# The modulation of a two-block transformer: from TensorE products to running sums on VectorE and GpSimd

## The reference, cut to what matters

```python
silu_c = jax.nn.silu(c)                 # 1 x 1024
silu_cc = jax.nn.silu(c_ctx)            # 1024
for l in range(2):
    mx = jnp.split((silu_c @ w_mod[l] + b_mod[l])[:, None, :], 6, axis=-1)    # w_mod[l] is 1024 x 6144
    mc = jnp.split(silu_cc @ w_mod[l] + b_mod[l], 6, axis=-1)
    zx = modulate(rms_norm_2(x, norm1_g[l]), mx[0], mx[1]) @ w_in[l]
    ...
```

## Time and profile before

| | |
|---|---|
| Median of 3 runs | 3625.23 us (3624.39 to 3630.41) |
| The profiled execution's own time | 3626.35 us |
| Its span, from first to last instruction | 3624.6 us |
| Mean granted TensorE clock | 0.996 |
| Busy: TensorE matmul, weight load | 97%, 74% |
| Busy: VectorE, ScalarE, GpSimd | 47%, 38%, 0% |
| The two stages with the modulation | from about 645 to 1023 us and from about 1649 to 2029 us |

### The profile page before, as it was taken

How to read it: one execution, slowest core, us unless ns; L and a number is a source line. 1 busy time by engine, 2 the same in 40 slices (tenths; PEclk the granted TensorE clock), 3 DMA queues, 4 the chain that set the end, 5 groups by cost and what they waited for, 6 DMA issues and landing times.

```text
span 3624.6 us, 47267 instructions
## 1 busy us (share of the span) xinstructions
PE 3527.7 (97%) x17969; PEld 2669.8 (74%) x17969; DVE 1721.4 (47%) x2508; ACT 1387.3 (38%) x2058; POOL 3.4 (0%) x11
## 2 busy tenths in 40 slices
PE   8999999999999989999999899999999999999999
PEld 5565788777775657887777765488888885469998
DVE  6674434433466754344334555543323355644334
ACT  5554323322245543233222334533322334443334
POOL 0000000000000000000000000000000000000000
PEclk9999999999999999999999999999999999999999
DMA  4121233555532222335555310022222221013332
GB/s 127 54 62 50 84 90 108 145 155 148 145 101 58 57 58 79 93 115 156 149 164 155 81 49 3 2 58 65 64 64 63 59 82 58 4 51 95 93 93 88
DMA packets 576207, 310.28 MB, mean 86 GB/s; under 512 B 28400, under 2 KB 566976, under 8 KB 576064
## 3 DMA queue, kind: packets, MB, share of 16 engines
q1 hardware_dynamic: 575792, 308.18, 30.3%
q10 hardware_dynamic: 272, 0.13, 0.0%
HBM read 297.26 MB, written 2.10 MB: 83 GB/s over the span
## 4 chain that ended last, share of the span: by engine, by line
PE 93%; DVE 3%; ACT 2%; issue 1%; DMA 0%; SPq 0%; DVEq 0%; ACTq 0%
PE ps L1111 14%; PE ps L1112 14%; PE ps L1113 14%; PE ps L1420 10%; PE ps L1422 10%; PE ps L1424 10%; PE ps L1608 2%; PE ps L1590 2%; PE ps L1301 2%; PE ps L1270 1%; PE ps L1195 1%; PE ps L1282 1%; PE ps L1549 1%; PE ps L1298 1%; PE ps L1276 1%
## 5 line engine op out<-in xcount | busy, mean ns | idle before, releaser
L1772 ACT ACTIVATE whi<-wraw 128x1024 fp32r<-128x1024 f32 x448 | 470.7, 1052 | 552.4 <-DMA wraw<-in_w_mlp 247.2
L1111 PE MATMUL ps<-uhi,whi 128*128 128x512 f32 (+1 forms) x1456 | 613.5, 421 | 12.5 <-DVE ulo L2431 5.4
L2414 DVE TENSOR_TENSOR wlo<-wraw,whi 128x1024 fp32r<-128x1024 f32 x448 | 546.0, 1219 | 109.1 <-ACT whi L1772 104.2
L1112 PE MATMUL ps<-ulo,whi 128*128 128x512 f32 (+1 forms) x1456 | 572.7, 393 | 0.0
L1113 PE MATMUL ps<-uhi,wlo 128*128 128x512 f32 (+1 forms) x1456 | 572.5, 393 | 0.0
L1111 PEld LDWEIGHTS ps<-uhi,whi 128*128 128x128 f32 x1456 | 274.2, 188 | 103.0 <-issue 38.6
L1112 PEld LDWEIGHTS ps<-ulo,whi 128*128 128x128 f32 x1456 | 274.7, 189 | 72.3 <-issue 16.3
L1113 PEld LDWEIGHTS ps<-uhi,wlo 128*128 128x128 f32 x1456 | 273.8, 188 | 65.4
L1420 PE MATMUL ps<-u2hi,whi 128*128 128x512 f32 (+1 forms) x1216 | 295.6, 320 | 3.3 <-DVE wlo L2414 2.4
L1420 PE MATMUL ps<-yhi,whi 128*128 128x512 f32 (+1 forms) x976 | 295.9, 353 | 0.0
L1422 PE MATMUL ps<-ylo,whi 128*128 128x512 f32 (+1 forms) x976 | 294.9, 353 | 0.0
(11 more groups left out here) (329 smaller groups left out, 4567.9 us busy)
## 6 DMA issues: line engine op xcount, KB each, us to landing
wraw<-in_w_in SPq DMA_DIRECT2D x128, 512.0 KB, 3.8
wraw<-in_w_mlp SPq DMA_DIRECT2D x128, 512.0 KB, 4.0
mod_raw<-in_w_mod SPq DMA_DIRECT2D x96, 512.0 KB, 5.3
wraw<-in_w_mlp_in SPq DMA_DIRECT2D x64, 512.0 KB, 4.2
wraw<-in_w_mlp_out SPq DMA_DIRECT2D x64, 512.0 KB, 3.9
wraw<-in_w_branch SPq DMA_DIRECT2D x16, 512.0 KB, 3.4
wraw<-in_w_out SPq DMA_DIRECT2D x16, 512.0 KB, 3.8
wraw<-in_w_o SPq DMA_DIRECT2D x16, 512.0 KB, 3.7
```

Source lines behind the costliest of these rows:

```text
L1111: pe.matmul(bank, whs[:, i], x_hi[:, k], start=(i == 0), stop=False)
L1112: pe.matmul(bank, whs[:, i], x_lo[:, k], start=False, stop=False)
L1772: act.activation(whi[:, r], wraw[:, r], ACT.Copy).then_inc(w_hi, 1)
L2414: dve.tensor_tensor(wlo[:, r], wraw[:, r], whi[:, r].bitcast(F32), ALU.subtract).then_inc(w_split, 1)
```

## The change

The sum over the 1024 rows of `w_mod` is split: over the 8 feature tiles k it is made as multiply-and-add of whole tiles (128 x 384), with the partition's value of the condition as a scalar; over the 128 partitions it is made by six transposes on TensorE and a `tensor_reduce` over 128 values on VectorE. VectorE makes the sum for the first condition (one multiplication, then seven `scalar_tensor_tensor`, each behind the one before), GpSimd that for the second (one multiplication, then seven pairs of multiplication and addition, each step behind the one before: 15 steps a group). The loads are now pieces of 3, 3 and 2 feature tiles with all 384 columns (rows of 1536 bytes); SyncE waits for VectorE's sums of the piece (`mod_added`) before it loads the next group's piece into its place. VectorE takes piece b after chunk b = 0, 1, 2, once GpSimd has done with it (`mod_step`). TensorE turns both sums (six transposes, banks `SCORE` and `SCORE + 1`) after chunk b = 3, once both are whole; GpSimd begins the next group behind that (`mod_turned`). The sums lie in `acc`, which is free during the MLP. `mod_kept` now counts the `tensor_reduce` of each group, and TensorE waits for it ahead of the next use of the banks.

```diff
--- before.py
+++ after.py
@@ -84,6 +84,8 @@
 
 UNIT_START, UNIT_SPACE = 18, 2.85
 MOD_GROUP = 3
+MOD_PIECES = ((0, 3), (3, 6), (6, 8))
+MOD_STEPS = 2 * 8 - 1
 BRANCH_TILES = {"diff": (0, 1, 2, 3), "ret": (11, 8, 9, 10), "gqa": (4, 5, 6, 7)}
 BRANCH_KINDS = "diff", "ret", "gqa"
 RET_UNITS, RET_SCORES = (25, 30), (119.5, 134)
@@ -625,7 +627,7 @@
         par_dw = sb("par_dw", [P, DEPTH * TAPS * 2])
         mod = sb("mod", [P, DEPTH, MOD_COLS, 2])
         silu = sb("silu", [P, KT, 2])
-        silu_parts = sb("silu_parts", [P, KT, 32])
+        silu_parts = sb("silu_parts", [P, KT, 2])
 
         one_scope = ExitStack()
         h = sb("h", [P, KT, SEQ], scope=one_scope)
@@ -686,9 +688,10 @@
         sb("place_of_fsq", [P, SEQ], scope=merge_scope)
         sgm = sb("sgm", [P, 2, SEQ], scope=merge_scope)
         acc = sb("acc", [P, 2, SEQ], scope=merge_scope)
+        mod_sums = acc[:, :, SEQ - MOD_GROUP * P:SEQ]
         mst = sb("mst", [P, 2, SEQ], scope=merge_scope)
-        mod_raw = sb("mod_raw", [P, MOD_GROUP, KT, P], scope=merge_scope)
-        mod_rows = sb("mod_rows", [P, MOD_GROUP * P], scope=merge_scope)
+        mod_raw = sb("mod_raw", [P, KT, MOD_GROUP * P], scope=merge_scope)
+        mod_part = sb("mod_part", [P, MOD_GROUP * P], scope=merge_scope)
         merge_scope.close()
         one_scope.close()
 
@@ -795,7 +798,8 @@
         second_in, static_in, dft_in = sem("second_in"), sem("static_in"), sem("dft_in")
         silu_sig_ready, silu_ready = sem("silu_sig_ready"), sem("silu_ready")
         mod_in = [sem(f"mod_in{b}") for b in range(MOD_GROUP)]
-        mod_made, mod_kept, mod_turned = sem("mod_made"), sem("mod_kept"), sem("mod_turned")
+        mod_step, mod_kept, mod_turned = sem("mod_step"), sem("mod_kept"), sem("mod_turned")
+        mod_added = sem("mod_added")
         ring_done, mid_evac = sem("ring_done"), sem("mid_evac")
         early_done, early_added, early_squared = sem("early_done"), sem("early_added"), sem("early_squared")
         early_summed, early_normed, early_log = sem("early_summed"), sem("early_normed"), sem("early_log")
@@ -947,10 +951,11 @@
                                 sp.dma_start(wraw[:, r, :].rearrange("p (k c) -> p k c", c=P), src)\
                                   .then_inc(raw_in[r], 16)
                                 if w_mod is not None and n:
-                                    c = P * MOD_GROUP * (2 * KT // RAW * q + i) + P * (MOD_GROUP * KT // RAW * half + n - 1)
-                                    made = MOD_GROUP * (2 * KT // RAW * q + i)
-                                    sp.wait_ge(mod_made, made + (l * MOD_COLS + MOD_GROUP * KT // RAW * half + n))
-                                    sp.dma_start(mod_raw[:, n - 1], w_mod[:, :, bass.ds(c, P)])\
+                                    group = 2 * KT // RAW * q + i + KT // RAW * half
+                                    k, end = MOD_PIECES[n - 1]
+                                    sp.wait_ge(mod_added, KT * group + (MOD_COLS // MOD_GROUP * KT * l + end))
+                                    sp.dma_start(mod_raw[:, k:end],
+                                                 w_mod[:, k:end, bass.ds(MOD_GROUP * P * group, MOD_GROUP * P)])\
                                       .then_inc(mod_in[n - 1], 16)
 
                 if w_mod is not None and l == DEPTH - 1:
@@ -1083,9 +1088,31 @@
                                pattern=[[-1, P]], channel_multiplier=1).then_inc(pool_const, 1)
             pool.wait_ge(pool_const, 3)
             pool.memset(rotated[:, :], 0.0).then_inc(rotated_clear, 1)
-            pool.wait_ge(mod_turned, 2 * KT // RAW * QUARTERS)
+            groups = MOD_COLS // MOD_GROUP
+
+            def mod_products(l):
+
+                for g in range(groups * l, groups * (l + 1)):
+                    pool.wait_ge(mod_turned, g + 1)
+                    for b, (first, end) in enumerate(MOD_PIECES):
+                        pool.wait_ge(mod_in[b], 16 * g + 16)
+                        for k in range(first, end):
+                            by, n = silu_parts[:, k, 1:2], MOD_STEPS * g + 2 * k - 1
+                            if k == 0:
+                                pool.tensor_scalar(mod_sums[:, 1], mod_raw[:, k], by, None, ALU.mult).then_inc(mod_step, 1)
+                            else:
+                                pool.wait_ge(mod_step, n)
+                                pool.tensor_scalar(mod_part[:, :], mod_raw[:, k], by, None, ALU.mult).then_inc(mod_step, 1)
+                                pool.wait_ge(mod_step, n + 1)
+                                pool.tensor_tensor(mod_sums[:, 1], mod_sums[:, 1], mod_part[:, :], ALU.add)\
+                                    .then_inc(mod_step, 1)
+
+            pool.wait_ge(silu_ready, 1)
+            mod_products(0)
+            pool.wait_ge(mod_turned, 2 * KT // RAW * QUARTERS + 1)
             pool.memset(rotated[:, :], 0.0).then_inc(rotated_clear, 1)
-            pool.wait_ge(mod_turned, 2 * KT // RAW * QUARTERS * DEPTH)
+            mod_products(1)
+            pool.wait_ge(mod_turned, 2 * KT // RAW * QUARTERS * DEPTH + 1)
             pool.memset(columns[:, :], 0.0).then_inc(second_const, 1)
             pool.wait_ge(second_const, 1)
             pool.memset(k2[QK:QK + 1, :, :], 1.0).then_inc(second_const, 1)
@@ -1185,25 +1212,18 @@
                 pe.transpose(out[:, 0:96], prow2[0:96, 0, :], ident[0:96, 0:96])
                 pe.transpose(out[:, P:P + 124], prow2[0:124, 1, :], ident[0:124, 0:124]).then_inc(params_turned, 1)
 
-            def mod_product(b, group):
-
-                pe.wait_ge(mod_in[b], 16 * group + 16)
-                pe.wait_ge(mod_kept, MOD_GROUP * group + (b + 1))
-                for half in range(2):
-                    for lane in range(4):
-                        k = 4 * half + lane
-                        last = pe.matmul(ps[32 * lane:32 * (lane + 1), SCORE + b, 0:P], silu_parts[:, k, :],
-                                         mod_raw[:, b, k], start=(half == 0), stop=(half == 1))
-                last.then_inc(mod_made, 1)
-
             def mod_turn(group):
 
-                pe.wait_ge(mod_kept, MOD_GROUP * group + 2 * MOD_GROUP)
-                for c in range(MOD_GROUP):
-                    last = pe.transpose(ps[:, ATT, P * c:P * (c + 1)], mod_rows[:, P * c:P * (c + 1)], ident[:, :])
+                pe.wait_ge(mod_step, MOD_STEPS * group + MOD_STEPS)
+                pe.wait_ge(mod_added, KT * group + 2 * KT)
+                pe.wait_ge(mod_kept, group + 1)
+                for v in range(2):
+                    for c in range(MOD_GROUP):
+                        last = pe.transpose(ps[:, SCORE + v, P * c:P * (c + 1)], mod_sums[:, v, P * c:P * (c + 1)], ident[:, :])
                 last.then_inc(mod_turned, 1)
 
-            pe.sem_inc(mod_made, MOD_GROUP)
+            pe.sem_inc(mod_turned, 1)
+
             def half_norm(n):
 
                 pe.wait_ge(sq_used, n.sq + n.tiles)
@@ -1230,6 +1250,7 @@
             for s in plan.layers:
                 if s.layer:
                     first_pair(s.norm1)
+                    pe.wait_ge(mod_kept, MOD_COLS // MOD_GROUP * s.layer + 1)
                 for step in s.heads:
                     if s.layer and step.name in ("part", "project") and (
                             step.head if step.name == "part" else step).chunk < s.norm1.chunk + 2:
@@ -1335,8 +1356,6 @@
                 if s is plan.layers[-1]:
                     turn_context()
 
-                pe.wait_ge(silu_ready, 1)
-
                 def up_or_down(q, half, i, b):
                     chunk, tile = s.mlp.chunk + KT * half + b, s.mlp.tile + KT * half + b
                     made = {k: (m_lo, KT * q + (s.mlp.tile_m + max(k, 5) + 3)) for k in (0, 6, 7)}
@@ -1348,10 +1367,7 @@
 
                 def mods(q, half, i, b):
                     group = 2 * KT // RAW * q + i + (2 * KT // RAW * QUARTERS * s.layer + KT // RAW * half)
-                    if b == RAW - 2:
-                        for c in range(MOD_GROUP):
-                            mod_product(c, group)
-                    elif b == RAW - 1:
+                    if b == RAW - 1:
                         mod_turn(group)
 
                 pe.wait_ge(w_split, s.mlp.chunk + 2)
@@ -1465,6 +1481,7 @@
 
             for s in plan.second:
                 if s.layer == 0:
+                    pe.wait_ge(mod_kept, MOD_COLS // MOD_GROUP * DEPTH + 1)
                     wide_norm(s.norm1)
                 pe.wait_ge(static_in, 64 * (s.layer + 1) + 16)
                 pe.wait_ge(second_const, 2)
@@ -2367,7 +2384,8 @@
                 dve.wait_ge(dve_linked, links[0])
 
 
-            dve.sem_inc(mod_kept, MOD_GROUP)
+            dve.sem_inc(mod_kept, 1)
+            dve.sem_inc(mod_added, KT)
             for j in range(KT):
                 dve.wait_ge(h_in, j + 1)
                 buffer_wait(dve, sq_used, j)
@@ -2676,15 +2694,21 @@
                 def mods(b, l, group):
 
```

(24 more changed lines are left out.)

## The result

The changed kernel takes 3655.62 us (median of 4 runs, 3653.62 to 3657.53) where the kernel before took 3625.86 us in 4 runs beside it: a ratio of 1.008, 95% interval 1.0062 to 1.0097. It is slower by 30 us. The forecast was 3588, the range ended at 3652.

The account below looks back on a forecast made before the run. The prediction took TensorE, busy 97% of the span, as the bound. It saved 41.9 us over 32 groups, less 4.0 at the ends: 37.9 off the profiled 3626.35 us, said as 3588, range 3581 to 3652.

Parts of the forecast that it names:

- TensorE's saving: In the MLP groups, six transposes replace the products: 1.31 us saved a group, group at 23.05, 41.9 us over 32 groups.
- VectorE's 5.3 us at nothing: VectorE's added multiply-adds and reduce, 5.3 us a group, were costed at nothing because its idle time covers them.
- GpSimd's step, 0.90 us: Mean step of GpSimd's 15-step chain in a group, handover included: 0.90 us, bounds 0.74 and 1.51; stall taken as 0.
- the 1.36 at which TensorE would stand still: Longest GpSimd step, in us, that the group could hold before TensorE stands still at the turn.
- The formula for the group: If GpSimd's chain sets the group, its length is 15 t + 2.65 us for step t, deciding from t = 1.45.
- The rival "slower": GpSimd's chain sets the MLP group: 3658 us at step 1.51, 3654 with port waits, 3702 at 1.6; chance 0.20.
- The port as a rival of its own: VectorE and GpSimd wait for each other's large reads; up-half groups give back 29 us, 3600 to 3617; chance 0.15.
- an estimate of 0.84 us for the addition: GpSimd's addition of 384 elements, scaled from the skill's 4497 ns for 2048 f32; the sum itself took 0.85.
- Places in memory at nothing: The tiles' new memory positions were said to cost nothing.
- The ends, 4.0 us: Time given back where the layers' MLPs begin and end: 2.2 and 0.8 in layer 0, 0.95 in layer 1, together 4.0.
- The sum's 2.2 at the end of layer 0: At layer 0's end the last group's 1.64 us is given back and the turn begins 0.55 later: 2.2 us.

Follow-up runs that it names:

- e1: Changed kernel with GpSimd making only one multiplication a piece (3 of 15 operations a group), second sum incomplete: 3598.69 us, 0.9924 of the kernel before.
- e8: Changed kernel with memsets for GpSimd's 15 steps, of undisturbed lengths in layer 0, short in layer 1; second sum left out: 3598.13 us.
- e9: Changed kernel with VectorE waiting for the load instead of GpSimd's steps, and the next load waiting for both: 3635.94 us, 1.0028 of the kernel before.
- e16: Changed kernel with memsets for GpSimd's steps, in layer 0 meant to match the disturbed mean lengths, layer 1 short; second sum left out: 3613.13 us.
- e2: Changed kernel with GpSimd running one group ahead, a second place for its sum, and inner MLP loops written out on TensorE: 3611.83 us.
- e7: The changed kernel with GpSimd a group ahead, plus 240 unused words behind `silu_parts`, so later tiles keep their addresses from before the change: 3606.16 us.
- e11: Changed kernel with VectorE adding the last two tiles of both sums, GpSimd making 11 steps, and the old addresses kept: 3620.69 us.

## Why the prediction was wrong

Going by its own steps:

- **TensorE's saving** held. With the chain out of the way the turns stand at 23.07 us (forecast 23.05), no row of TensorE reads `mod_raw`, and six transposes cost what was said.
- **VectorE's 5.3 us at nothing** held in size (0.62 a multiply-add, 0.95 the reduce, undisturbed) and in e1, e8. It failed through the order of its queue. VectorE waits for GpSimd's steps, so its last two multiply-adds stand behind the chain (1.5 us a group), and at the end of layer 0 its `wlo` and the norm's sum do, for which TensorE waited 5.6 us. Removing this gave 19.7 us (e9).
- **GpSimd's step, 0.90 us,** is the step that failed. I priced the multiplication at 0.51 from the select's row and it takes 1.25, more than an addition; the addition takes 1.02, for 0.85 (the select's fixed part, which went into it as 0.12, is 0.18 by the same rows; rounded, that gives the same); the handover 0.09, for 0.23. Undisturbed a step is (8 x 1.25 + 7 x 1.02) / 15 + 0.09 = 1.23 us, under the 1.36 at which TensorE would stand still, and e8 shows that such a chain costs nothing. The stretching beside VectorE took it from there to (358.1 + 49.2 + 251.3) / (32 x 15) + 0.09 = 1.46 us. The formula for the group then gives 15 x 1.46 + 2.65 = 24.6 us, near the 24.7 of the turns. The rival "slower" had this very case, a step of 1.25 and 1.5 with port waits, and its chance of 0.20 was too low, because my central step of 0.90 came from a row of another operation. That its 3654 us is within 2 us of the 3655.6 is luck in part: with the measured 1.46 the same sum gives 3625 + 32 x 0.2 + 4 = 3635, and the rest is what it hadn't in it, the places in memory (5.7) and the layers' ends.
- **The port as a rival of its own** had the contention right and not what it does: it filled a group with both engines' demands (22.6 of 23.05 us) and gave back to 3600 to 3617, with 6 us of slack for GpSimd. GpSimd had about 2, and the stretching made its chain, one step behind the other, 3.7 us longer. The Trainium skill, SBUF — State Buffer, section Who interferes with whom, states that a VectorE instruction with two SBUF inputs and a GpSimd instruction that reads SBUF exclude each other. The runs agree: `wlo` 1.22 against 2.03 us, a multiplication 1.25 against 2.32, and no such pairs when GpSimd only writes (e8, e16). The Trainium skill, GPSIMD Engine Reference, section Performance versus the Vector engine, led to an estimate of 0.84 us for the addition; it took 1.02.
- **Places in memory at nothing** was wrong by 5.7 us (e2 against e7).
- **The ends, 4.0 us,** were too low. Between e8 and the forecast lie 10.1 us, 5.7 of them the addresses; the remaining 4.4 I put to the ends, which makes 8.4, as a remainder and not measured. Most of it shows in e8's turns: about 1.6 us before the first one (the sum had the start of an MLP at 0, at most 2; from run to run this stretch differs by 1 us and more), and 1.8 in the last two groups of layer 1, of 24.6 and 23.4 us. The sum's 2.2 at the end of layer 0 came true. Where the chain disturbs, the ends cost more: 27.5 us for the change's last group of layer 0, the 5.6 us wait for the norm's sum in it, and 28.0 and 25.7 for the last two of layer 1.

Summed: 3588 + 5.7 (addresses) + 4.4 (ends) + 57.5 (GpSimd's reading chain, the change against e8) = 3655.6. The 4.4 is what the other terms leave. Of the 57.5, 54.5 lie between the turns (28.2 in layer 0, 26.3 in layer 1): about 44 in the ordinary groups, by the chain's length, and 10.5 in the last group of layer 0 and the last two of layer 1. How these last divide between the chain and VectorE's queue is not shown, nor what the lower clock cost there.

## What to carry to other kernels

A dependent chain on a second engine costs its whole length beside a busy neighbour, with what starts it and what stands behind it, as soon as that is more than the group: before giving GpSimd the last word ahead of a TensorE step, time one of the very instructions it will run, with VectorE busy beside it, and let it run a group ahead, which brought more here (43.8 us) than shortening its operations (23.7) or its number of steps (29, e11 less the 5.7 of the addresses). An engine that must do other urgent work shouldn't wait in its queue for a slower one only to free a buffer; let the loader wait for both. And when a tile changes size, compare a stage that the change doesn't touch: places alone moved TensorE's rate by 0.9%.

## What the runs showed of the hardware

- On GpSimd a multiplication of 128 x 384 f32 by a scalar column took 1.25 us undisturbed, longer than the sum or the product of two such tensors (1.02 and about 1.0); a memset of 384 elements would take an estimated 0.42, between the 0.19 for 128 and the 0.52 for 512.
- Beside VectorE's operations with two inputs in SBUF, GpSimd's multiplications took up to 2.6 us for 1.25, its additions up to 2.1 for 1.02, VectorE's `wlo` up to 2.05 for 1.22. Memsets of 1.00 to 1.58 us, which read nothing, lengthened nothing.
- Matmuls with unchanged operands, shapes and clock start every 174.5 or 176.1 ns, by where the tiles lie in SBUF (2292 against 2272 in 400 us). A shift of 896 bytes had yet another pattern: fast in the second block (2289), 0.3% slower in the MLP (groups of 23.14 us for 23.06).
- In layer 0 of the change the granted clock fell to its lower level beside the four turns ahead of which TensorE had been idle for 2.16 to 2.36 us. In layer 0 of e9 and e16, with at most 1.0 us idle ahead of a turn, it stayed at the upper level up to the last group.
